# Feed-forward input stages with weights stationary and 256 tokens moving, for 18 of 22 weight groups

## The chip, the core and the metric

The kernel runs on one core of a Trainium2 chip. The metric is the device time of one execution in microseconds (us); three runs of the kernel before gave 941.71, 942.28 and 942.32 us, median 942.28.

## The reference

256 tokens of 1024 channels, all in float32, pass through a first block (feed-forward, token mixing by retention and neighbourhood attention, feed-forward) and a second block (a gated linear recurrence, a gated short convolution), with an RMS norm ahead of each part. The change touches the two feed-forward parts alone, which compute

```python
def _swiglu(x, w_in, w_out):
    g, u = jnp.split(x @ w_in, 2, axis=-1)
    return (jax.nn.silu(g) * u) @ w_out

for l in range(DEPTH):
    h = _swiglu(_rms_norm(x, ffn1_pre_norm[l]), ffn1_w_in[l], ffn1_w_out[l])
    x = x + 0.5 * _rms_norm(h, ffn1_post_norm[l])
    # token mixing
    h = _swiglu(_rms_norm(x, ffn2_pre_norm[l]), ffn2_w_in[l], ffn2_w_out[l])
    x = x + 0.5 * _rms_norm(h, ffn2_post_norm[l])
```

`w_in` is 1024 x 5632 (2816 gate columns and 2816 up columns) and `w_out` is 2816 x 1024.

## The kernel before

The program streams all weights once, in groups of 128 partitions x 2048 float32 (1 MB), through a ring of 4 slots. SyncE loads `raw`; ScalarE rounds it to `w_hi` (type fp32r); VectorE subtracts and gives `w_lo`. Every product of the large matrices is the sum of three matmuls in fp32r, hi times hi, hi times lo and lo times hi, so that the result keeps float32 precision. The normed tokens lie transposed in `xT_hi` and `xT_lo`, 8 blocks of 128 channels x 256 tokens.

In the feed-forward input stages (`f1_in`, `f2_in`, 22 groups each) two groups hold one column: 512 output columns (256 of the gate, 256 of the up part) over all 1024 channels. `column_tile` does one of the two halves of the tokens, t = 0 or 1, with 24 matmuls by `product`: a 128 x 128 piece of `xT` is the stationary operand and 512 columns of the weights move past it. So results stand in PSUM (`acc[:, t, par]`) with tokens on partitions. ScalarE takes silu of the gate half (`silu_g`), VectorE multiplies by the up half (`prod`), and because the next product needs the hidden channels on partitions, TensorE transposes `prod` with four 128 x 128 transposes per column (`hidden_transposes`, into the PSUM banks `aux`). ScalarE then rounds the transposed block to `hT_hi` and VectorE makes `hT_lo`. The output stages (`f1_out`, `f2_out`) use `hT` as stationary operand in the same way (`out_stage`).

All order is written by hand: each engine has its own program, and they meet at semaphores. A weight slot is given back to ScalarE when TensorE has used it (the table `RELEASE`), and the columns 2 to 9 of an input stage are a hardware loop of two columns per pass (`column`); column 10 follows outside it. TensorE starts a column tile once VectorE has emptied its PSUM bank two columns earlier, and does the transposes of the column before between the two tiles of a column. An input stage has 11 columns and 11 such bursts of four transposes; the last burst stands behind the first block of the output stage.

The weight load of a matmul is no instruction of the program here: the built rows show a matmul alone, the trace shows a LDWEIGHTS with each.

Of the kernel before, what the change touches and what calls it, by code (L numbers as in the profile page):

```python
# [53 lines left out]
ACC_READERS = {"f1_in": "V" * 11, "f1_out": "V", "mix_in": "AAAVVAAVVAAAA", "na_out": "V", "mix_out": "V",  # L54
               "f2_in": "V" * 11, "f2_out": "V", "a_in": "AAAVVV", "a_out": "V", "b_in": "V" * 12, "b_out": "V"}
ACC_ORDER = "".join(ACC_READERS.values())
FIRST_ACC = {}
for _name in ACC_READERS:
# [3 lines left out]
FILL_COUNTS = [("t0", 4), ("f1_in", 11), ("t1", 4), ("nq", 2), ("nk", 2), ("rq", 2), ("rk", 2), ("rs", 4), ("rp", 4),  # L62
               ("yna", 2), ("yret", 4), ("merged", 4), ("t2", 4), ("f2_in", 11), ("t3", 4),
# [3 lines left out]
SPLIT_COUNTS = [("t0", 4), ("f1_in", 11), ("t1", 4), ("yna", 2), ("yret", 4), ("merged", 4), ("t2", 4),  # L67
                ("f2_in", 11), ("t3", 4), ("gate", 6), ("t4", 4), ("b_in", 12)]
# [35 lines left out]
def build(nc, weights, x_in, gains, ident_in, rot_in, colmask_in, dist_in, decay_in, lam_in, bias_in, gate_w_in,  # L104
          gate_b_in, conv_a_in, conv_ab_in, conv_b_in, out):
    with ExitStack() as ctx:
# [60 lines left out]
        prod = at("prod", [P, 2, T, 256], F32, area + 47104)  # L167

# [53 lines left out]
        gate_ready = [sem(f"gate_ready{t}") for t in range(T)]  # L222
        bank_full = sem("bank_full")
# [59 lines left out]
        def act_frees(t, instruction):  # L283
            instruction.then_inc(acc_free_act[t], 1)

# [131 lines left out]
        def _(act):  # L417
# [4 lines left out]
            def round_group(g, slot=None, wait_used=True):  # L422
# [4 lines left out]
                if g >= RING:  # L427
                    kind, n = RELEASE[g - RING]
                    act.wait_ge({"used": group_used, "acc": acc_full[1], "ret": ret_acc_full}[kind], n)
# [7 lines left out]
            def round_in_loop(base_group, i, i0, b, per=4):  # L437
# [5 lines left out]
                act.wait_ge({"used": group_used, "acc": acc_full[1]}[kind], i * (per // 2) + (n - i0 * (per // 2)))  # L443
# [78 lines left out]
            def swiglu(which, normed):  # L522
# [16 lines left out]
                def column(j, par, rounds):  # L539
                    rounds()  # L540
                    silu(j, par, 0)
                    if not (isinstance(j, int) and j == 0):
                        hidden_hi(j - 1, 1 - par)
                    silu(j, par, 1)
# [17 lines left out]
                split[0] += 16  # L562
                column(10, 0, lambda: round_to(g0 + 24))
                round_to(g0 + 25)
                hidden_hi(10, 0)
# [9 lines left out]
            gates = [11, 11]  # L575
# [226 lines left out]
        def _(dve):  # L802
# [117 lines left out]
            def swiglu(which):  # L920
# [18 lines left out]
                def column(j, par, lows):  # L939
                    lows()  # L940
                    up(j, par, 0)
                    if not (isinstance(j, int) and j == 0):
                        hidden_lo(j - 1, 1 - par)
                    up(j, par, 1)
# [14 lines left out]
                with dve.Fori(1, 5) as i:  # L959
                    for b in range(2):  # L960
                        column(i * 2 + b, b, lambda: [low_in_loop(g0 + 6, i, 1, 2 * b + h) for h in range(2)])
                split[0] += 16
                column(10, 0, lambda: low_to(g0 + 24))
                low_to(g0 + 25)
                hidden_lo(10, 0)
                low_to(FIRST_GROUP[f"{which}_out"] + GROUPS[f"{which}_out"])

            GATES_F2 = 11 + 2
# [27 lines left out]
            for c in range(13):  # L996
                for t in range(T):
# [29 lines left out]
                    if c in (7, 8):  # L1027
                        dve.wait_ge(gate_ready[t], 11 + c - 6)
# [102 lines left out]
            gate0 = GATES_F2 + 11  # L1131
# [100 lines left out]
            gate0 = GATES_F2 + 11 + 3  # L1232
# [65 lines left out]
        def _(pe):  # L1298
# [64 lines left out]
            def out_stage(st, hi, lo, chunks, wait_chunk=lambda n: None, after_first=lambda: None, norm=None,  # L1363
                          last=3):
# [4 lines left out]
                for block in blocks:  # L1369
                    for t in range(T):  # L1370
                        if block[0] == 0:
                            wait_acc_free(pe, t, FIRST_ACC[st])
                        for n in block:
# [37 lines left out]
            def swiglu(which, n):  # L1411
# [26 lines left out]
                with pe.Fori(1, 5) as i:  # L1438
                    for b in range(2):
# [228 lines left out]
def _stream(inputs):  # L1668
# [6 lines left out]

    def rows(w):
        return w.reshape(-1, 2, P, DM).transpose(0, 2, 1, 3).reshape(-1, P, GROUP)

    def blocks(parts, width, at):
# [4 lines left out]
    ff = blocks((0, 1), 256, (0, FF))  # L1684
# [10 lines left out]
        columns(a["ffn1_w_in"][0], ff), rows(a["ffn1_w_out"][0]), columns(a["w_mix_in"][0], mix),  # L1695
        rows(a["w_na_out"][0]), rows(a["w_ret_out"][0]), rows(a["w_mix_out"][0]),
        columns(a["ffn2_w_in"][0], ff), rows(a["ffn2_w_out"][0]), columns(a["a_w_in_2"][0], a_cols),
# [62 lines left out]
```

## Time and profile before

| | |
|---|---|
| median of three runs | 942.28 us |
| profiled execution, first to last instruction | 940.6 us |
| TensorE matmul records, busy | 910.5 us, 97% |
| TensorE weight loads, busy (beside the matmuls) | 748.2 us, 80% |
| VectorE, ScalarE, GpSimd busy | 563.0, 451.7, 80.4 us |
| granted TensorE clock, mean over the span | 0.994 |
| HBM traffic | 167.61 MB read, 179 GB/s over the span |

The profile gives no time of the profiled execution other than its span; the runs' median lies 1.7 us above that span. In the timeline a row gives the start in us, the time to the end of the last instruction in it, the engine, the line, the operation with its tiles, and in brackets what it waited for. The end of a matmul is modelled and overlaps the next ones, so that the time of one matmul is read from the distance between two starts. PEld is the weight load; it has its own rows.

### The profile page before, as it was taken

The page shows a single profiled execution, that of the slowest core. Times are in us where ns is not written, and L with a number is a line of the kernel's source. Part 1 is how long each engine was busy: PE and PEld are TensorE (multiplying, and loading weights), DVE is VectorE, ACT ScalarE, POOL GpSimd, SP SyncE. Part 2 cuts the span into 40 slices and gives each one's busy share as a digit, 9 for nine tenths or more (in the row PEclk, how much of TensorE's full clock was granted, in tenths as well). Part 3 has the DMA queues.
Part 4 walks back from the last instruction along what each step waited for, and adds up shares of the span by engine and source line. Part 5 has one row for each costly group of instructions (what it writes and reads, how often), then busy time and mean ns, then how long its engine had stood idle before and what let it go on. Part 6 is the DMA issues. An engine that isn't in the chain of part 4 may idle for free.

```text
span 940.6 us, 11364 instructions
## 1 busy us (share of the span) xinstructions
PE 910.5 (97%) x4160; PEld 748.2 (80%) x4160; DVE 563.0 (60%) x625; ACT 451.7 (48%) x541; POOL 80.4 (9%) x107
## 2 busy tenths in 40 slices
PE   4999999999999999999999999999999799999997
PEld 3888888878888888888788888887887578888885
DVE  4755444466766556567655553555949866666653
ACT  5644444354533445436544443344877354444441
POOL 3000000003232200000000000000361200000000
PEclk9999999999999999999999999999999899999999
DMA  9744553637644443444544453755433454444421
GB/s 345 245 185 194 194 197 140 250 130 257 214 171 163 169 154 138 154 159 179 223 179 178 178 186 134 300 202 182 170 123 117 152 192 182 185 178 178 178 90 45
DMA packets 25684, 169.18 MB, mean 180 GB/s; under 512 B 3392, under 2 KB 3568, under 8 KB 6448
## 3 DMA queue, kind: packets, MB, share of 16 engines
q1 hardware_dynamic: 22752, 159.92, 45.7%
q0 software_dynamic: 2752, 8.69, 2.8%
q8 instruction: 25, 0.41, 0.2%
q14 instruction: 11, 0.09, 0.0%
q10 hardware_dynamic: 144, 0.07, 0.0%
HBM read 167.61 MB, written 1.05 MB: 179 GB/s over the span
## 4 chain that ended last, share of the span: by engine, by line
PE 89%; DVE 4%; ACT 3%; issue 2%; DMA 1%; SPq 0%; DVEq 0%; ACTq 0%
PE acc L1305 27%; PE acc L1307 26%; PE acc L1306 26%; DMA raw<-weights 1%; DVE w_lo L810 1%; PE aux L1425 1%; PE aux L1606 1%; PE aux L1358 1%; ACT w_hi L430 1%; PE aux L1306 1%; PE aux L1305 1%; PE aux L1307 1%; PE aux L1468 1%; PE aux L1518 1%; PE aux L1485 1%
## 5 line engine op out<-in xcount | busy, mean ns | idle before, releaser
L810 DVE TENSOR_TENSOR w_lo<-raw,w_hi 128x2048 fp32r<-128x2048 f32 x147 | 334.9, 2302 | 150.4 <-ACT w_hi L430 116.0
L1305 PE MATMUL acc<-w_hi,xT_hi 128*128 128x512 f32 x880 | 351.6, 400 | 6.0 <-DVE w_lo L810 3.0
L1307 PE MATMUL acc<-w_hi,xT_lo 128*128 128x512 f32 x880 | 344.7, 392 | 0.0
L1306 PE MATMUL acc<-w_lo,xT_hi 128*128 128x512 f32 x880 | 343.8, 391 | 0.0
L430 ACT ACTIVATE w_hi<-raw 128x2048 fp32r<-128x2048 f32 x97 | 184.0, 1912 | 91.1 <-PE acc L1307 75.9
L1305 PEld LDWEIGHTS acc<-w_hi,xT_hi 128*128 128x128 f32 x880 | 165.9, 188 | 41.3 <-DVE w_lo L810 4.7
L1307 PEld LDWEIGHTS acc<-w_hi,xT_lo 128*128 128x128 f32 x880 | 165.7, 188 | 35.8
L1306 PEld LDWEIGHTS acc<-w_lo,xT_hi 128*128 128x128 f32 x880 | 166.1, 189 | 32.8
L444 ACT ACTIVATE w_hi<-raw 128x2048 fp32r<-128x2048 f32 x52 | 96.6, 1910 | 0.9 <-issue 0.9
L532 ACT ACTIVATE silu_g<-acc 128x256 f32<-128x256 f32 x44 | 16.9, 383 | 121.5 <-PE acc L1307 121.5
L1305 PE MATMUL acc<-w_hi,hT_hi 128*128 128x512 f32 x176 | 69.8, 396 | 0.0
L1307 PE MATMUL acc<-w_hi,hT_lo 128*128 128x512 f32 x176 | 69.4, 395 | 0.0
L1306 PE MATMUL acc<-w_lo,hT_hi 128*128 128x512 f32 x176 | 69.4, 394 | 0.0
L930 DVE TENSOR_TENSOR prod<-acc,silu_g 128x256 f32<-128x256 f32 x44 | 18.5, 421 | 76.8 <-ACT silu_g L532 76.8
L1305 PE MATMUL acc<-w_hi,yT_hi 128*128 128x512 f32 x96 | 39.6, 413 | 5.8 <-DVE yT_lo L841 5.8
L1307 PEld LDWEIGHTS acc<-w_hi,hT_lo 128*128 128x128 f32 x176 | 33.2, 188 | 7.7
L1306 PEld LDWEIGHTS acc<-w_lo,hT_hi 128*128 128x128 f32 x176 | 33.2, 189 | 7.6
L1307 PE MATMUL acc<-w_hi,yT_lo 128*128 128x512 f32 x96 | 39.2, 408 | 0.0
L1305 PEld LDWEIGHTS acc<-w_hi,hT_hi 128*128 128x128 f32 x176 | 33.2, 188 | 7.5
L1306 PE MATMUL acc<-w_lo,yT_hi 128*128 128x512 f32 x96 | 39.1, 408 | 0.0
L581 ACT ACTIVATE prob<-neg_s,neg_max 128x256 f32<-128x256 f32 x16 | 8.2, 510 | 52.3 <-DVE neg_max L1067 41.6
L449 ACT ACTIVATE xT_hi<-aux 128x512 fp32r<-128x512 f32 x24 | 13.4, 596 | 33.9 <-PE aux L1358 28.6
(176 smaller groups left out, 774.2 us busy)
## 6 DMA issues: line engine op xcount, KB each, us to landing
raw<-weights SPq DMA_DIRECT2D x149, 1024.0 KB, 4.9
gain_pre<-gains POOLq DMA_DIRECT2D x5, 512.0 KB, 6.8
bias_raw<-bias_in POOLq DMA_DIRECT2D x32, 64.0 KB, 2.3
gain_post<-gains POOLq DMA_DIRECT2D x3, 512.0 KB, 6.1
gate_w<-gate_w_in POOLq DMA_DIRECT2D x1, 1536.0 KB, 7.0
x<-x_in SPq DMA_DIRECT2D x2, 512.0 KB, 8.0
raw<-weights SPq DMA_DIRECT2D x2, 512.0 KB, 7.8
out<-tmp SPq DMA_DIRECT2D x4, 256.0 KB, 2.1
```

The costliest lines, as they stand in the source:

```text
L430: a.activation(w_hi[:, slot], raw[:, slot], ACT.Copy).then_inc(hi_done, 1)
L444: a.activation(w_hi[:, slot], raw[:, slot], ACT.Copy).then_inc(hi_done, 1)
L449: a.activation(dst, source if source is not None else aux[:, bank], ACT.Copy, scale=scale)\
L532: a.activation(silu_g[:, t], acc[:, t, par, 0:256], ACT.Silu).then_inc(gate_ready[t], 1)
L810: v.tensor_tensor(w_lo[:, slot], raw[:, slot], w_hi[:, slot].bitcast(F32), ALU.subtract)\
L930: v.tensor_tensor(prod[:, par, t], acc[:, t, par, 256:512], silu_g[:, t], ALU.mult)\
L1305: m.matmul(dst, hi[:, k, cols], w_hi[:, slot, w], start=first, stop=False)
L1306: m.matmul(dst, hi[:, k, cols], w_lo[:, slot, w], start=False, stop=False)
L1307: return m.matmul(dst, lo[:, k, cols], w_hi[:, slot, w], start=False, stop=last)
L1358: i = m.transpose(aux[:, 2 * t + h, c * P:(c + 1) * P], tmp[:, t, (4 * h + c) * P:(4 * h + c + 1) * P], ident[:])
L1425: i = m.transpose(aux[:, par, c * S + t * P:c * S + (t + 1) * P], prod[:, par, t, c * P:(c + 1) * P], ident[:])
L1468: m.matmul(aux[:, 1, 0:S], nqT[h % 2][:, h // 2, t * P:(t + 1) * P], nkT[:, h // 2, :], start=True, stop=True).then_inc(s_full, 1)
```

## The change

The first 4 of the 22 groups (two columns) of each feed-forward input stage stay as they were (`STRAIGHT = 4`). The other 18 groups (`TURNED = 18`) are laid out anew in memory: a group now holds 128 gate columns and 128 up columns over all 1024 channels, a chunk. For a chunk TensorE takes a 128 x 128 piece of the weights as the stationary operand and lets the 256 tokens of `xT` move past it, 3 x 8 matmuls for the gate half and as many for the up half, both into one PSUM bank (`turned_bank`). The result has hidden channels on partitions. ScalarE takes silu (`silu_c`), VectorE multiplies (`prod_c`, in SBUF), ScalarE rounds `prod_c` to `hT_hi` and VectorE subtracts for `hT_lo`. No transposes are needed for these chunks. Four chunk banks take turns; a chunk waits for the product of the chunk four before it.

On TensorE, inside the loop of `f1_in`: before, the middle of one column (L1305 to L1307 are the three matmuls of `product`, L1425 the transposes)

```order
L1305 MATMUL acc<-w_hi,xT_hi 128x512
L1306 MATMUL acc<-w_lo,xT_hi 128x512
L1307 MATMUL acc<-w_hi,xT_lo 128x512
L1422 REGISTER_ALU
L1425 MATMUL aux<-ident,prod 128x128 x4
L1305 MATMUL acc<-w_hi,xT_hi 128x512
L1306 MATMUL acc<-w_lo,xT_hi 128x512
L1307 MATMUL acc<-w_hi,xT_lo 128x512
```

and now, the end of one chunk and the start of the next (L1507 to L1509 are the three matmuls of `turned_chunk`)

```order
L1507 MATMUL acc<-xT_hi,w_hi 128x256
L1508 MATMUL acc<-xT_lo,w_hi 128x256
L1509 MATMUL acc<-xT_hi,w_lo 128x256
L1497 REGISTER_ALU
L1501 REGISTER_ALU
L1507 MATMUL acc<-xT_hi,w_hi 128x256
L1508 MATMUL acc<-xT_lo,w_hi 128x256
L1509 MATMUL acc<-xT_hi,w_lo 128x256
```

The transposes are gone from the loop, and a group has 48 matmuls of 256 columns where it had 24 of 512. On ScalarE the loop of `f1_in` holds, before, for one column (two groups)

```order
L444 ACTIVATE w_hi<-raw 128x2048 x2
L529 REGISTER_ALU
L532 ACTIVATE silu_g<-acc 128x256
L535 REGISTER_ALU
L537 ISA
L537 ACTIVATE hT_hi<-aux 128x512
L532 ACTIVATE silu_g<-acc 128x256
```

and now, for two chunks (two groups)

```order
L465 ACTIVATE w_hi<-raw 128x2048
L567 ACTIVATE silu_c<-acc 128x256
L574 ISA
L574 ACTIVATE hT_hi<-prod_c 128x256
L465 ACTIVATE w_hi<-raw 128x2048
L567 ACTIVATE silu_c<-acc 128x256
L574 ISA
L574 ACTIVATE hT_hi<-prod_c 128x256
```

One rounding of 512 columns out of PSUM has become two of 256 out of SBUF; VectorE's loop changes in the same way. The diff, without the counts of semaphores that follow from it:

```diff
+STRAIGHT = 4
+TURNED = 18
+TURNED_BEFORE = {"f1_in": 0, "f2_in": TURNED}
 ...
-        if _name.endswith("_in") and _g % 2 or _name.endswith("_out") and _g == _n - 1:
+        if _name in TURNED_BEFORE and _g >= STRAIGHT:
+            RELEASE.append(("turned", TURNED_BEFORE[_name] + _g - STRAIGHT + 1))
+        elif _name.endswith("_in") and _g % 2 or _name.endswith("_out") and _g == _n - 1:
 ...
+        def turned_bank(b):
+            return acc[:, 1 - b % 4 // 2, b % 2]
 ...
+                def chunk_silu(n, b):
+                    act.wait_ge(turned_full, n + (c_before + 1))
+                    if not (isinstance(n, int) and n < 2):
+                        act.wait_ge(prod_ready, n + (c_before - 1))
+                    a.activation(silu_c[:, b % 2], turned_bank(b)[:, 0:S], ACT.Silu).then_inc(silu_ready, 1)
+
+                def chunk_round(n, b):
+                    act.wait_ge(prod_ready, n + (c_before + 1))
+                    ...
+                    a.activation(dst, prod_c[:, b % 2], ACT.Copy).then_inc(chunk_hi, 1)
 ...
-                with act.Fori(1, 5) as i:
-                    for b in range(2):
-                        column(i * 2 + b, b, lambda: [round_in_loop(g0 + 6, i, 1, 2 * b + h) for h in range(2)])
+                with act.Fori(1, 4) as i:
+                    for b in range(4):
+                        round_in_loop(g0 + 10, i, 1, b)
+                        chunk_silu(i * 4 + b, b)
+                        chunk_round(i * 4 + (b - 1), b + 3)
 ...
+                def chunk_up(n, b):
+                    dve.wait_ge(silu_ready, n + (c_before + 1))
+                    ...
+                    v.tensor_tensor(prod_c[:, b % 2], turned_bank(b)[:, S:2 * S], silu_c[:, b % 2], ALU.mult)\
+                        .then_inc(prod_ready, 1)
+
+                def chunk_low(n, b):
+                    dve.wait_ge(chunk_hi, n + (c_before + 1))
+                    ...
+                    v.tensor_tensor(dst, prod_c[:, b % 2], hi.bitcast(F32), ALU.subtract).then_inc(chunk_lo, 1)
 ...
-                def column(j, par):
-                    for t in range(T):
-                        pe.wait_ge(acc_free_dve[t], n_dve - 1 + j)
-                        column_tile(g0 + 2 * j, (g0 + 2 * par) % RING, par, t)
-                        if t == 0:
-                            hidden_transposes(j - 1, 1 - par)
+                def turned_chunk(c, b):
+                    pe.wait_ge(lo_done, c + (g0 + STRAIGHT + 1))
+                    if isinstance(c, int) and c < 4:
+                        pe.wait_ge(acc_free_dve[1 - c // 2], n_dve + 1 + c % 2)
+                    else:
+                        pe.wait_ge(prod_ready, c + (c_before - 3))
+                    slot = (g0 + STRAIGHT + b) % RING
+                    for half in range(2):
+                        dst = turned_bank(b)[:, half * S:(half + 1) * S]
+                        for k in range(KD):
+                            w = slice(2 * P * k + P * half, 2 * P * k + P * (half + 1))
+                            m.matmul(dst, w_hi[:, slot, w], xT_hi[:, k, :], start=k == 0, stop=False)
+                            m.matmul(dst, w_hi[:, slot, w], xT_lo[:, k, :], start=False, stop=False)
+                            i = m.matmul(dst, w_lo[:, slot, w], xT_hi[:, k, :], start=False, stop=k == KD - 1)
+                    i.then_inc(turned_full, 1)
 ...
-                with pe.Fori(1, 5) as i:
-                    for b in range(2):
-                        column(i * 2 + b, b)
-                column(10, 0)
+                for c in range(4):
+                    turned_chunk(c, c)
+                    if c == 0:
+                        hidden_transposes(1, 1)
+                with pe.Fori(1, 4) as i:
+                    for b in range(4):
+                        turned_chunk(i * 4 + b, b)
+                for c in range(16, TURNED):
+                    turned_chunk(c, c)
 ...
-                    pe.wait_ge(bank_free, f0 + g + 1)
-
-                out_stage(f"{which}_out", hT_hi, hT_lo, FF // P, wait_chunk, lambda: hidden_transposes(10, 0),
-                          n + 1, 4)
+                    if g < STRAIGHT // 2:
+                        pe.wait_ge(bank_free, f0 + g + 1)
+                    else:
+                        pe.wait_ge(chunk_lo, c_before + 2 * g - STRAIGHT + 2)
+
+                def free_banks(t):
+                    pe.wait_ge(prod_ready, c_before + (TURNED if t else TURNED - 2))
+
+                out_stage(f"{which}_out", hT_hi, hT_lo, FF // P, wait_chunk, lambda: None, n + 1, 4, free_banks)
```

## Rows read from the trace of the kernel before

**Rows 1.** The page: busy time by engine, granted TensorE clock, last chain by engine.

```profile
PE 910.5 (97%) x4160; PEld 748.2 (80%) x4160; DVE 563.0 (60%) x625; ACT 451.7 (48%) x541; POOL 80.4 (9%) x107
PEclk9999999999999999999999999999999899999999
PE 89%; DVE 4%; ACT 3%; issue 2%; DMA 1%; SPq 0%; DVEq 0%; ACTq 0%
```

**Rows 2.** All that TensorE waited for: us in total, times, longest us.

```profile
PE aux L1358 <- DVE tmp L878: 9.3, 3, 8.0
PE acc L1305 <- DVE yT_lo L841: 5.8, 2, 3.8
PE acc L1305 <- DVE w_lo L810: 3.0, 3, 1.0
PE acc L1305 <- DVE w_lo L826: 3.0, 1, 3.0
PE aux L1595 <- DVE a_stage L1183: 2.1, 1, 2.1
```

**Rows 3.** Timeline of TensorE, transposes of successive columns: f1_in, then f2_in (columns as above).

```profile
56.96 0.60 PE L1425 MATMUL aux<-ident,prod 128*128 128x128 f32 x4
68.33 0.60 PE L1425 MATMUL aux<-ident,prod 128*128 128x128 f32 x4
...
136.57 0.60 PE L1425 MATMUL aux<-ident,prod 128*128 128x128 f32 x4
...
472.18 0.60 PE L1425 MATMUL aux<-ident,prod 128*128 128x128 f32 x4
...
563.16 0.60 PE L1425 MATMUL aux<-ident,prod 128*128 128x128 f32 x4
```

**Rows 4.** Timeline of TensorE, matmuls of 512 columns ahead of and behind a burst.

```profile
99.73 0.39 PE L1305 MATMUL acc<-w_hi,xT_hi 128*128 128x512 f32 x1
...
102.45 0.60 PE L1425 MATMUL aux<-ident,prod 128*128 128x128 f32 x4
102.81 0.48 PE L1305 MATMUL acc<-w_hi,xT_hi 128*128 128x512 f32 x1
103.12 0.40 PE L1306 MATMUL acc<-w_lo,xT_hi 128*128 128x512 f32 x1
```

**Rows 5.** Timeline of the weight loads (PEld) around the same burst.

```profile
102.22 0.58 PEld L1425 LDWEIGHTS aux<-ident,prod 128*128 128x128 f32 x4
102.78 0.19 PEld L1305 LDWEIGHTS acc<-w_hi,xT_hi 128*128 128x128 f32 x1
102.89 0.19 PEld L1306 LDWEIGHTS acc<-w_lo,xT_hi 128*128 128x128 f32 x1
103.12 0.19 PEld L1307 LDWEIGHTS acc<-w_hi,xT_lo 128*128 128x128 f32 x1
```

**Rows 6.** Timeline of TensorE, 16 transposes in a row, in mix_in.

```profile
375.95 1.04 PE L1459 MATMUL aux<-ident,y_na 128*128 128x128 f32 x8
376.83 1.04 PE L1459 MATMUL aux<-ident,y_ret 128*128 128x128 f32 x8
```

**Rows 7.** Timeline of TensorE, 8 passes of a plain float32 matmul of 256 columns.

```profile
330.71 1.89 PE L1518 MATMUL aux<-rv,decay 128*128 128x256 f32 x8
332.44 0.59 PE L1468 MATMUL aux<-nkT,nqT 128*128 128x256 f32 x2
```

**Rows 8.** Timeline of the weight loads, matmuls of 64 columns, then the first of 512.

```profile
260.58 0.53 PEld L1485 LDWEIGHTS aux<-nv,probT 128*128 128x128 f32 x4
261.03 0.19 PEld L1305 LDWEIGHTS acc<-w_hi,xT_hi 128*128 128x128 f32 x1
```

**Rows 9.** Timeline of TensorE in f1_out, at 512 columns: the first and twelfth of twelve.

```profile
157.58 0.39 PE L1305 MATMUL acc<-w_hi,hT_hi 128*128 128x512 f32 x1
...
160.13 0.40 PE L1307 MATMUL acc<-w_hi,hT_lo 128*128 128x512 f32 x1
```

**Rows 10.** Groups by line, 45.6 to 136.5 us: busy, mean ns | idle before.

```profile
L810 DVE TENSOR_TENSOR w_lo<-raw,w_hi 128x2048 fp32r<-128x2048 f32 x17 | 38.2, 2288 | 12.3 <-ACT w_hi L444 10.9 <-ACT w_hi L430 1.4
L444 ACT ACTIVATE w_hi<-raw 128x2048 fp32r<-128x2048 f32 x14 | 26.0, 1908 | 0.9 <-issue 0.9
L1306 PEld LDWEIGHTS acc<-w_lo,xT_hi 128*128 128x128 f32 x128 | 24.1, 188 | 4.8
L930 DVE TENSOR_TENSOR prod<-acc,silu_g 128x256 f32<-128x256 f32 x16 | 6.7, 421 | 31.8 <-ACT silu_g L532 31.8
L532 ACT ACTIVATE silu_g<-acc 128x256 f32<-128x256 f32 x16 | 6.1, 383 | 48.6 <-PE acc L1307 48.6
L936 DVE TENSOR_TENSOR hT_lo<-aux,hT_hi 128x512 f32 x8 | 5.4, 680 | 0.0
L537 ACT ACTIVATE hT_hi<-aux 128x512 f32 x8 | 4.8, 598 | 1.3 <-PE aux L1425 1.3
```

More of the change, by code:

```diff
@@ L167, in build @@
         prod = at("prod", [P, 2, T, 256], F32, area + 47104)
+        silu_c = at("silu_c", [P, 2, S], F32, area + 51200)
+        prod_c = at("prod_c", [P, 2, S], F32, area + 53248)
         nqT = [at(f"nqT{i}", [P, NH // 2, S], F32, area + 4096 * i) for i in range(2)]
@@ L428, in round_group @@
                     kind, n = RELEASE[g - RING]
[L429 removed]
+                    act.wait_ge({"used": group_used, "acc": acc_full[1], "ret": ret_acc_full,
+                                 "turned": turned_full}[kind], n)
                 a.activation(w_hi[:, slot], raw[:, slot], ACT.Copy).then_inc(hi_done, 1)
@@ L442, in round_in_loop @@
                 kind, n = RELEASE[base_group + b - RING]
-                act.wait_ge({"used": group_used, "acc": acc_full[1]}[kind], i * (per // 2) + (n - i0 * (per // 2)))
+                each = per if kind == "turned" else per // 2
+                act.wait_ge({"used": group_used, "acc": acc_full[1], "turned": turned_full}[kind],
+                            i * each + (n - i0 * each))
                 a.activation(w_hi[:, slot], raw[:, slot], ACT.Copy).then_inc(hi_done, 1)
@@ L537, in hidden_hi @@
                     a.activation(dst, aux[:, par].rearrange("p (c q) -> p c q", c=2), ACT.Copy).then_inc(bank_hi, 1)
[L539 to L544, printed above, removed]
+                c_before = TURNED_BEFORE[st]
+                def chunk_silu(n, b):
[5 more added lines that the diff above has]
+                    act.wait_ge(prod_ready, n + (c_before + 1))
+                    dst = hT_hi[:, STRAIGHT + n, :] if isinstance(n, int) else \
+                        hT_hi[:, bass.ds(n + STRAIGHT, 1), :].rearrange("p a q -> p (a q)")
+                    a.activation(dst, prod_c[:, b % 2], ACT.Copy).then_inc(chunk_hi, 1)
                 if g0 == 0:
@@ L937, in hidden_lo @@
                                     hT_hi[:, chunks, :].bitcast(F32), ALU.subtract).then_inc(bank_free, 1)
[L939 to L944, printed above, removed]
+                c_before = TURNED_BEFORE[st]
+                def chunk_up(n, b):
+                    dve.wait_ge(silu_ready, n + (c_before + 1))
+                    if not (isinstance(n, int) and n < 2):
+                        dve.wait_ge(chunk_lo, n + (c_before - 1))
+                    v.tensor_tensor(prod_c[:, b % 2], turned_bank(b)[:, S:2 * S], silu_c[:, b % 2], ALU.mult)\
+                        .then_inc(prod_ready, 1)
+                def chunk_low(n, b):
+                    dve.wait_ge(chunk_hi, n + (c_before + 1))
+                    dst, hi = (hT_lo[:, STRAIGHT + n, :], hT_hi[:, STRAIGHT + n, :]) if isinstance(n, int) else \
+                        [x[:, bass.ds(n + STRAIGHT, 1), :].rearrange("p a q -> p (a q)") for x in (hT_lo, hT_hi)]
+                    v.tensor_tensor(dst, prod_c[:, b % 2], hi.bitcast(F32), ALU.subtract).then_inc(chunk_lo, 1)
                 if g0 == 0:
@@ L958, in swiglu @@
                 hidden_lo(0, 0)
-                with dve.Fori(1, 5) as i:
-                    for b in range(2):
-                        column(i * 2 + b, b, lambda: [low_in_loop(g0 + 6, i, 1, 2 * b + h) for h in range(2)])
-                split[0] += 16
-                column(10, 0, lambda: low_to(g0 + 24))
+                for n in range(4):
+                    low_to(g0 + 7 + n)
+                    chunk_up(n, n)
+                    if n == 0:
+                        hidden_lo(1, 1)
+                    else:
+                        chunk_low(n - 1, n - 1)
+                with dve.Fori(1, 4) as i:
+                    for b in range(4):
+                        low_in_loop(g0 + 10, i, 1, b)
+                        chunk_up(i * 4 + b, b)
+                        chunk_low(i * 4 + (b - 1), b + 3)
+                split[0] += 12
+                for n in range(16, TURNED):
+                    low_to(g0 + 7 + n)
+                    chunk_up(n, n)
+                    chunk_low(n - 1, n - 1)
+                chunk_low(TURNED - 1, TURNED - 1)
                 low_to(g0 + 25)
-                hidden_lo(10, 0)
                 low_to(FIRST_GROUP[f"{which}_out"] + GROUPS[f"{which}_out"])
-            GATES_F2 = 11 + 2
+            GATES_F2 = 2 + 2
             swiglu("f1")
@@ L1674, in columns, with chunks @@
         return w.reshape(-1, P, GROUP)
+    def chunks(w, order):
+        w = w.reshape(KD, P, -1)[:, :, order]
+        return w.transpose(2, 1, 0, 3).reshape(-1, P, GROUP)
     def rows(w):
```

54 lines of the change are left out of this document (36 added, 18 removed).

## The prediction, made before the result was known

> **What bounds the kernel now.** I read the page first. TensorE's matmul records cover 97% of the span and make up 89% of the chain that ended last [rows 1]. The list of its waits comes to 23 us in the whole kernel, and none of it is in the part of the feed-forward input stages that changes: its largest entries belong to the norms (L1358), to the recurrence (L841) and to the start (L826) [rows 2]. The groups by line for the loop of `f1_in` say the same from the other side: VectorE and ScalarE sit idle there for silu and for matmul results, 48.6 us before silu alone in 91 us, and no TensorE group idles [rows 10]. So inside these stages the time is a count of TensorE instructions times their pitch, the distance between two starts. Everything else only has to keep up.
>
> The pitch is what one must read with care. A matmul record of 512 columns is 390 ns long, but twelve of them start in 2.72 us (99.73 to 102.45), so the pitch is 227 ns [rows 4]. The granted clock is at its upper level, 2.4 GHz, in the feed-forward stages [rows 1], where 512 columns are 213 ns; 13 ns per matmul are something else. The same holds for the weight load: its record is 188 ns long [rows 10], yet loads follow each other faster than that (below).
>
> **What is removed and added on TensorE.** A column (two groups) takes 11.37 us: the bursts at 56.96 and 68.33 are that far apart, those from 56.96 to 136.57 are 7 x 11.37, and in the second stage 472.18 to 563.16 is 8 x 11.37 [rows 3]. 48 matmuls at 227 ns are 10.88 us of it; the other 0.49 us is the burst of four transposes with what it upsets: 0.36 us from its start to the next matmul's record, and 0.31 instead of 0.23 us from there to the one after [rows 4]. Nine columns of each stage are turned, and nine bursts of each go (the burst of column 1 stays, that of column 10 behind the first output block goes). Old time of what is replaced: 9 x 11.37 = 102.35 us per stage, 4.4 of it bursts.
>
> New time: 18 chunks x 48 = 864 matmuls of 256 columns per stage, each with a weight load of its own (the three rows of a chunk show the same slice of `w_hi` used twice in a row; the trace of before has a load record for every matmul, 4160 and 4160 [rows 1], although `xT_hi` is used twice in a row there too, so none will be saved). With a pitch p a stage takes 864 p. The change breaks even at p = 102.35 / 864 = 118.5 ns. This is the whole question: the same number of columns moves as before, but the fixed part of a matmul and the weight load are paid twice as often, against 4.4 us of bursts.
>
> **Bounds of p.** No fp32r matmul of 256 columns is in the trace. From below: weight loads limit it. Behind matmuls of 64 columns loads start every 112 ns (four from 260.58 to 261.03) [rows 8]; an fp32r load behind a short matmul is followed by the next after 0.11 us (102.78, 102.89) [rows 5]; 16 transposes keep 0.11 us each (8 from 375.95 to 376.83) [rows 6]. So p is at least 110 to 112 ns: now 0.23 us of matmul hides a load of 0.11, then they are about equal. That the load runs beside the matmul before it is seen in rows 5: the load at 102.89 starts as the matmul whose own load began at 102.78 begins, and the next matmul starts only at 103.12. From the matmul's side: 256 columns are 107 ns at 2.4 GHz. If the 13 ns grow with the columns (17/16 of 512), p is 113 ns; if they are paid per matmul, 120 ns. In the output stage the same shape has a pitch of 232 ns (eleven starts in 2.55 us), 19 ns extra [rows 9], which speaks for a cost per matmul that depends on what surrounds it, and would give 126 ns. From above: eight passes of plain float32 with 256 columns take 1.73 us, 216 ns each [rows 7], and the load's record is 188 ns [rows 10]; both would be reached only if a load could no more run beside the short matmul ahead of it, which rows 6 and 8 speak against.
>
> I take 120 ns: the extra varies between 13 and 19 ns at one and the same column count, so it is not a share of the columns, and plain float32, where the array needs two steps per column (216 for 213 ns), hardly shows it, so it is something of the full-rate stream at each start. Sum: 864 x 0.120 = 103.7 us against 102.35, +1.35 per stage, +2.7 us for both.
>
> A page of the Trainium skill, "TensorE: Matmul & The Clock Gate" (Back-to-back issue gap), gives the gap as columns / 2.4 plus 2.5 ns. The plain float32 rows agree (216); the fp32r rows do not (227 where it says 216), and the measurement decides. Its section LDWEIGHTS gives columns / 1.2, 107 ns for 128, and the rows above show 108 to 112.
>
> **The rest of the change.** VectorE per group: 2.29 + 0.42 for the product, and for `hT_lo` at most 0.68, its price for twice the elements: 3.4 us of a chunk of 5.4 to 5.8. ScalarE: 1.91 + 0.38 + at most 0.60 = 2.9 us [rows 10]. Both have cover, so I cost them at nothing; if the cover were gone, the excess over 5.7 us would be paid 36 times. The waits added: TensorE waits for the product of the chunk four before, whose silu and product (0.8 us plus what is queued ahead, one rounding or subtraction of 1.9 to 2.3) had three chunks, 17 us. The slot of a group is released when its chunk ends, and rounding 1.91 and subtracting 2.29 have three chunks too; queued behind it on ScalarE is the silu of a chunk that TensorE is still in. At the end of the stage the last chunk's bank is needed by t = 1 of the output stage, after 24 matmuls, 5.4 us, against about 1 us of silu and product, or 3.5 us if a subtraction stands ahead. SyncE's loads wait for `lo_done` as before, and the bytes are the same. Bound on all this: 0 to +2 us for a wait at the four seams, and to -1.3 us per output stage if its 232 ns fell to 227 for want of transposes (264 x 5 ns) [rows 9]; I take 0.
>
> 940.6 + 2.7 = 943.3 us of span, and with the 1.7 us between span and median of the runs, 945.0 us. I call changes within 0.2% (1.9 us) no difference, about what a measurement can tell.
>
> **Rivals.**
> First, the extra is not paid per matmul: a load and a matmul of about equal length run side by side and p is 110 to 116 ns. For it: loads and transposes do reach 110 to 112 [rows 5, 6, 8], and the 13 ns are exactly 1/16 of 213. Against it: rows 9. At 113.3 ns a stage takes 97.9 us, -4.4 each, 933.5 us; at 110, 95.0, -7.3 each, 927.7 us.
> The skill's gap rule (same page and section as above) says 109 ns for 256 columns; this rival is that rule with the load's limit from the rows.
>
> Second, p is larger, 123 to 135 ns: the load starts when the matmul ahead starts and needs 112 ns, and the extra of 13 to 19 ns comes behind whichever is later. For it: with both lengths near 110 there is no slack left between them, and [rows 9] show the larger extra for a whole stage of 512-column matmuls. It decides from p = 123 on. At 126 ns: 108.9 us, +6.5 each, 955.3 us; at 135 ns (112 and the larger extra, and a little): 116.6, +14.3 each, 970.9 us.
>
> Third, the short matmul hides no load, or TensorE's instruction supply falls behind over 864 in a row (the longest run of short ones in the trace is 16 [rows 6]): 188 ns gives 162.4, +60 each, 1062 us; 216 ns gives 186.6, 1111 us. The same page (Wait — 56ns, not 53.3ns?) has about 62 ns of sequencer time per MATMUL with hardware decode off; two instructions would be 124 ns, an estimate that falls in the second rival. No run here shows it.
>
> **How the numbers follow.** Forecast, 117.3 to 123 ns: 0.40, of which 0.10 falls within 0.2% (117.3 to 119.6 ns) and 0.30 above. First rival: 0.36, all faster. Second: 0.20. Third: 0.04. So faster 0.36, same 0.10, slower 0.54. The range leaves out the third rival, the far end of the second beyond 131 ns and the end of the first below 113: 932 to 964 us. The likeliest case alone is 940 to 950.
>
> **What would show it.** In the profile after, the pitch of `turned_chunk`'s matmuls: 24 of one half in 2.88 us, a chunk every 5.76 us. 5.4 us or less is the first rival, over 5.9 the second. The load records of these matmuls should start when the matmul ahead starts. Bursts of `prod` should be 16 instructions in all for the two stages, where there were 88. A wait of TensorE on `silu_c`, `prod_c` or `w_lo` of over 2 us in all in these stages would prove the costing of the rest wrong. I am wrong in sign if p is under 117.3 ns, and wrong in mechanism if TensorE idles between chunks.

## The result: 2.6 us slower, at the forecast pitch of 120 ns

The changed kernel takes 945.13 us (median of 19 runs, 944.28 to 947.64), the kernel before in the same comparison 942.55 us. The ratio is 1.0028, 95% interval 1.0021 to 1.0034. The forecast was 945.0 us. The profiled execution has a span of 942.9 us against 940.6.

The page of the changed kernel, busy time by engine, where [rows 1] stand for before:

```profile
PE 912.7 (97%) x4952; PEld 786.5 (83%) x4952; DVE 569.9 (60%) x643; ACT 452.4 (48%) x559; POOL 80.5 (9%) x107
```

There are 792 more matmuls and 792 more loads: 864 added (24 more for each of 36 groups), 72 transposes gone. TensorE has as few gaps as before. All its waits in the changed kernel (us in total, times, longest):

```profile
PE aux L1421 <- DVE tmp L919: 9.3, 3, 8.1
PE acc L1368 <- DVE yT_lo L882: 5.8, 2, 3.8
PE acc L1368 <- DVE w_lo L851: 3.1, 3, 1.1
PE acc L1368 <- DVE w_lo L867: 3.0, 1, 3.0
PE aux L1681 <- DVE a_stage L1246: 2.1, 1, 2.1
```

These are [rows 2] under new line numbers. No wait on a chunk's product or silu has come. So the whole difference must lie in TensorE's own work, the pitch of the new matmuls against that of the old ones and the bursts. The timeline of TensorE inside a chunk of `f1_in`, its first and ninth row of nine:

```profile
79.96 0.28 PE L1507 MATMUL acc<-xT_hi,w_hi 128*128 128x256 f32 x1
...
80.92 0.28 PE L1509 MATMUL acc<-xT_hi,w_lo 128*128 128x256 f32 x1
```

Eight distances in 0.96 us are 120.0 ns each. The weight loads keep the same beat and start with the matmul ahead of them, back to back (timeline of the loads, changed kernel):

```profile
79.96 0.19 PEld L1508 LDWEIGHTS acc<-xT_lo,w_hi 128*128 128x128 f32 x1
80.08 0.19 PEld L1509 LDWEIGHTS acc<-xT_hi,w_lo 128*128 128x128 f32 x1
```

Stage by stage, from the first burst to the first matmul of the output stage. Before, in `f1` and then in `f2`:

```profile
39.65 0.60 PE L1425 MATMUL aux<-ident,prod 128*128 128x128 f32 x4
...
142.51 0.40 PE L1305 MATMUL acc<-w_hi,hT_hi 128*128 128x512 f32 x1
...
466.24 0.60 PE L1425 MATMUL aux<-ident,prod 128*128 128x128 f32 x4
...
569.10 0.40 PE L1305 MATMUL acc<-w_hi,hT_hi 128*128 128x512 f32 x1
```

and in the changed kernel:

```profile
39.50 0.60 PE L1489 MATMUL aux<-ident,prod 128*128 128x128 f32 x4
...
144.04 0.39 PE L1368 MATMUL acc<-w_hi,hT_hi 128*128 128x512 f32 x1
...
467.37 0.60 PE L1489 MATMUL aux<-ident,prod 128*128 128x128 f32 x4
...
571.90 0.39 PE L1368 MATMUL acc<-w_hi,hT_hi 128*128 128x512 f32 x1
```

Second stage: 102.86 us before, 104.53 us after, +1.67. The first stage is the same (39.65 to 142.51, 39.50 to 144.04: +1.68). The last burst stood behind this point and is gone too, 0.49 us per stage. 2 x (1.67 - 0.49) = 2.4 us, against the span's 2.3.

### The profile page after: what moved, and what is told of

Read it like the earlier page. It is cut to its first block, busy times and chain, and to the rows that moved or that the text cites. A ratio compares the mean times of both kernels' runs of the same rounds, so it can differ in the third digit from the quotient of the medians.

```text
span 942.9 us, 12924 instructions
## 1 busy us (share of the span) xinstructions
PE 912.7 (97%) x4952; PEld 786.5 (83%) x4952; DVE 569.9 (60%) x643; ACT 452.4 (48%) x559; POOL 80.5 (9%) x107
## 4 chain that ended last, share of the span: by engine, by line
PE 89%; DVE 4%; ACT 3%; issue 2%; DMA 1%; SPq 0%; DVEq 0%; ACTq 0%
PE acc L1368 20%; PE acc L1370 19%; PE acc L1369 19%; PE acc L1508 7%; PE acc L1507 7%; PE acc L1509 7%; DMA raw<-weights 1%; DVE w_lo L851 1%; PE aux L1692 1%; PE aux L1421 1%; ACT w_hi L449 1%; PE aux L1368 1%; PE aux L1370 1%; PE aux L1369 1%; PE aux L1554 1%
## 5 line engine op out<-in xcount | busy, mean ns | idle before, releaser
L1368 PE MATMUL acc<-w_hi,xT_hi 128*128 128x512 f32 x592 | 237.4, 401 | 6.1 <-DVE w_lo L851 3.1
L1370 PE MATMUL acc<-w_hi,xT_lo 128*128 128x512 f32 x592 | 232.0, 392 | 0.0
L1369 PE MATMUL acc<-w_lo,xT_hi 128*128 128x512 f32 x592 | 231.6, 391 | 0.0
L1507 PE MATMUL acc<-xT_hi,w_hi 128*128 128x256 f32 x576 | 163.3, 284 | 0.0
L1509 PE MATMUL acc<-xT_hi,w_lo 128*128 128x256 f32 x576 | 163.0, 283 | 0.0
L1508 PE MATMUL acc<-xT_lo,w_hi 128*128 128x256 f32 x576 | 163.0, 283 | 0.0
L1368 PEld LDWEIGHTS acc<-w_hi,xT_hi 128*128 128x128 f32 x592 | 111.8, 189 | 30.8 <-DVE w_lo L851 4.9
L1369 PEld LDWEIGHTS acc<-w_lo,xT_hi 128*128 128x128 f32 x592 | 111.9, 189 | 22.0
L1508 PEld LDWEIGHTS acc<-xT_lo,w_hi 128*128 128x128 f32 x576 | 110.6, 192 | 0.0
L1507 PEld LDWEIGHTS acc<-xT_hi,w_hi 128*128 128x128 f32 x576 | 110.6, 192 | 0.0
L1509 PEld LDWEIGHTS acc<-xT_hi,w_lo 128*128 128x128 f32 x576 | 110.6, 192 | 0.0
```

The lines of the kernel that those rows point to most:

```text
L1368: m.matmul(dst, hi[:, k, cols], w_hi[:, slot, w], start=first, stop=False)
L1369: m.matmul(dst, hi[:, k, cols], w_lo[:, slot, w], start=False, stop=False)
L1370: return m.matmul(dst, lo[:, k, cols], w_hi[:, slot, w], start=False, stop=last)
L1507: m.matmul(dst, w_hi[:, slot, w], xT_hi[:, k, :], start=k == 0, stop=False)
L1508: m.matmul(dst, w_hi[:, slot, w], xT_lo[:, k, :], start=False, stop=False)
L1509: i = m.matmul(dst, w_lo[:, slot, w], xT_hi[:, k, :], start=False, stop=k == KD - 1)
```

## The experiments

Twelve kernels ran. They ask three things: whether each half of the sum has its size; what the 13 ns per matmul are; and why the same shape runs at 227 ns in one stage and 232 in another, on which the choice of 120 ns rested.

**The gain half alone.** The kernel before without nine bursts per stage; their waits and their signal stay:

```diff
-                        column_tile(g0 + 2 * j, (g0 + 2 * par) % RING, par, t)
-                        if t == 0:
-                            hidden_transposes(j - 1, 1 - par)
+                        column_tile(g0 + 2 * j, (g0 + 2 * par) % RING, par, t,
+                                    in_last=(lambda: hidden_waits(j - 1)) if t == 0 else None)
 ...
```

> The kernel before, in which the nine bursts of four transposes of the loop and column 10 of each feed-forward input stage are left out and only their waits and their signal remain (so the hidden layer of these columns is not right). This is the gain half of the change alone. My sum: 9 x 0.49 us per stage, 8.8 us in all, a ratio of 0.9906. Rival: the transposes fill time that TensorE would otherwise spend waiting for silu and product, so that less than half of it comes back: 0.995 or above. Second rival: only the array time of the transposes goes (36 x 0.107 per stage, 7.7 us) and the longer pitch behind them stays: 0.992.

933.83 us, ratio 0.9907 (0.9891 to 0.9924): 8.8 us, the size of my sum. 0.995 lies outside the interval, so the transposes did not fill idle time. The second rival's 0.992 lies inside it, but the trace tells the two apart. ScalarE's `silu_g` comes twice per column; its first and seventeenth row in the loop of `f1_in`, in this run:

```profile
45.70 0.38 ACT L532 ACTIVATE silu_g<-acc 128x256 f32<-128x256 f32 x1 [1.29 <-PE acc L1307]
...
132.74 0.38 ACT L532 ACTIVATE silu_g<-acc 128x256 f32<-128x256 f32 x1 [1.43 <-PE acc L1307]
```

Eight columns take 87.04 us, 10.88 each, where it was 11.37 [rows 3]. A burst was thus worth 0.49 us, as in my sum, and not only the 0.43 us of its four transposes (4 x 0.107).

The cost half follows: 1.0028 / 0.9907 = 1.0122, 11.4 us, where my sum has 2 x (103.68 - 97.9) = 11.5 us. The change is thus a trade of 11.4 against 8.8 us.

**Width of the moving operand, below 256.** In `turned_chunk`, `n` is 240 in the gate half and 192 in the up half:

```diff
+                        n = (240, 192)[half]
 ...
-                            m.matmul(dst, w_hi[:, slot, w], xT_hi[:, k, :], start=k == 0, stop=False)
+                            m.matmul(dst, w_hi[:, slot, w], xT_hi[:, k, 0:n], start=k == 0, stop=False)
 ...
```

> The changed kernel, with the moving operand of a chunk's matmuls cut to 240 of the 256 tokens in the gate half and to 192 in the up half (the last tokens of the hidden layer are left out, so the output is not the reference's). Theory A, a fixed 13.3 ns per fp32r matmul on top of columns / 2.4: 100.0 + 13.3 = 113.3 ns pitch at 240 columns; at 192 it would be 93.3, under the 110 to 112 ns that loads take, so 112 ns. Theory B, the 120 ns is the weight load (112 ns) plus a hand-over of 8 ns and has nothing to do with the columns: 120 ns at both. Theory C, the extra is a share of the columns plus the same load floor: 112 at both.

Timeline of TensorE in this run, the first and last row of 16 at 192 columns, then of 12 at 240:

```profile
60.17 0.27 PE L1510 MATMUL acc<-xT_hi,w_lo 128*128 128x192 f32 x1
...
61.85 0.28 PE L1510 MATMUL acc<-xT_hi,w_lo 128*128 128x192 f32 x1
...
62.20 0.27 PE L1510 MATMUL acc<-xT_hi,w_lo 128*128 128x240 f32 x1
...
63.43 0.28 PE L1509 MATMUL acc<-xT_lo,w_hi 128*128 128x240 f32 x1
```

112.0 ns at 192 columns and 111.8 at 240. Both lie at the distance of loads, 112 ns, and below 120, so the load is not what makes 120 (theory B falls). At 240 columns C said 112 and A 113.3. A is missed by 1.5 ns, more than the rounding of the two starts can make (0.9 ns): the 13.3 ns do not hold so close to the distance of loads.

**Width above 256.** The same with 320 and 384 columns.

> The changed kernel, with the moving operand of a chunk's matmuls made 320 columns wide in the gate half and 384 in the up half (they run into the next block of channels, and overlap in the PSUM bank, so the output is not the reference's). Theory A, 13.3 ns per matmul: 133.3 + 13.3 = 146.7 ns at 320 and 160 + 13.3 = 173.3 ns at 384. Theory C, 1/16 of the columns: 141.7 and 170.0 ns. Theory B (at 256 the load limits, and from some width on the columns): 142 to 147 and 170 to 173, it does not differ here. The span grows by 1728 matmuls x 40 ns = 69 us under A (mean pitch 160 against 120).

Timeline of this run, 18 rows at 384 columns and 20 at 320, first and last:

```profile
60.30 0.33 PE L1511 MATMUL acc<-xT_hi,w_hi 128*128 128x384 f32 x1
...
63.25 0.33 PE L1513 MATMUL acc<-xT_hi,w_lo 128*128 128x384 f32 x1
...
64.00 0.31 PE L1512 MATMUL acc<-xT_lo,w_hi 128*128 128x320 f32 x1
...
66.79 0.31 PE L1513 MATMUL acc<-xT_hi,w_lo 128*128 128x320 f32 x1
```

173.5 and 146.8 ns, where A had 173.3 and 146.7, and C 170.0 and 141.7. C falls here. Its 113 ns at 256 columns, one form of the prediction's first rival, had fallen with the measured 120.0. With a full load and the operands where they are, an fp32r matmul of 256, 320, 384 or 512 columns costs its columns at 2.4 GHz and 13.3 ns.

**Length of the load.** 64 of 128 weight columns as stationary operand, 256 and 192 columns moving:

```diff
-                        dst = turned_bank(b)[:, half * S:(half + 1) * S]
+                        n = (S, 192)[half]
+                        dst = turned_bank(b)[0:64, half * S:half * S + n]
 ...
-                            w = slice(2 * P * k + P * half, 2 * P * k + P * (half + 1))
+                            w = slice(2 * P * k + P * half, 2 * P * k + P * half + 64)
 ...
```

> The changed kernel, with 64 instead of 128 weight columns as stationary operand (64 of the 128 channels of each chunk are left out), 256 tokens moving in the gate half and 192 in the up half. The load is half as long. Theory A, the extra belongs to the start of the moving stream: 120.0 ns at 256 columns as before, and 80 + 13.3 = 93.3 ns at 192, since the load's floor falls from 112 to about 56 ns. Theory B, the pitch of 120 is load plus hand-over: both fall well under 120, to 107 to 110 at 256 columns and 80 to 83 at 192. Theory D, the extra is the load disturbing the stream beside it: it halves, 113.3 and 86.7 ns.

Timeline of this run, 21 rows at 192 columns, then 17 at 256, first and last:

```profile
60.24 0.25 PE L1508 MATMUL acc<-xT_hi,w_hi 128*64 128x192 f32 x1
...
62.01 0.25 PE L1510 MATMUL acc<-xT_hi,w_lo 128*64 128x192 f32 x1
...
62.92 0.28 PE L1509 MATMUL acc<-xT_lo,w_hi 128*64 128x256 f32 x1
...
64.73 0.28 PE L1510 MATMUL acc<-xT_hi,w_lo 128*64 128x256 f32 x1
```

88.5 and 113.1 ns. This is not A (93.3 and 120.0): of the 13.3 ns, 8.5 are left at 192 columns and 6.4 at 256, near theory D's 86.7 and 113.3. Two more runs tried D. The first takes 32 and 96 stationary columns at 256 moving; the second is the kernel before, with 64 token columns stationary in the groups that its hardware loop issues:

```diff
+                        rows = (32, 96)[half]
 ...
+                            w = slice(2 * P * k + P * half, 2 * P * k + P * half + rows)
```

```diff
+                        n = P if isinstance(g, int) else 64
 ...
+                        slot, cols, dst = (slot0 + half) % RING, slice(t * P, t * P + n), acc[0:n, t, par]
 ...
```

> The changed kernel, 256 tokens moving, with 32 stationary weight columns in the gate half and 96 in the up half (the other channels are left out). In the run with 64 stationary columns the pitch at 256 columns was 113.3 ns, at 128 it is 120.0. Theory D, the extra grows with the load's columns, 32 clock steps for 128: 32 columns 110.0 ns, 96 columns 116.7 ns. Rival, the extra comes in two steps (a short load gives 113.3, a long one 120.0): 113.3 and 120.0.

> The kernel before, in which the matmuls of the looped columns (columns 2 to 9 of the two feed-forward input stages, 2 to 11 of b_in; 1248 matmuls of 512 columns) have 64 instead of 128 stationary columns, so that half of the tokens' results in them are left out. It carries the finding of the run with half loads to the unturned form. Theory D, a load takes 32 clock steps from the stream it runs beside, a half load 16: the pitch falls from 226.7 to 220.0 ns, the span by 1248 x 6.7 = 8.3 us. Theory A, the extra is a start cost that only looked smaller in the short matmuls: 226.7 stays, and so does the span.

Timeline of the first of these runs, 21 rows with 96 stationary columns, then 21 with 32, first and last:

```profile
60.76 0.28 PE L1508 MATMUL acc<-xT_hi,w_hi 128*96 128x256 f32 x1
...
63.08 0.27 PE L1510 MATMUL acc<-xT_hi,w_lo 128*96 128x256 f32 x1
...
63.55 0.28 PE L1508 MATMUL acc<-xT_hi,w_hi 128*32 128x256 f32 x1
...
65.90 0.28 PE L1510 MATMUL acc<-xT_hi,w_lo 128*32 128x256 f32 x1
```

With 32 stationary columns the pitch was 117.5 ns, with 96 it was 116.0. D said 110.0 and 116.7, its rival 113.3 and 120.0; neither has both. In the unturned form with half loads the pitch rose, and the span with it, to 943.4 us (one run; the kernel before had 940.0 to 941.9 in the same comparison):

```profile
61.31 0.39 PE L1327 MATMUL acc<-w_hi,xT_lo 128*64 128x512 f32 x1
...
64.08 0.39 PE L1327 MATMUL acc<-w_hi,xT_lo 128*64 128x512 f32 x1
```

12 distances in 2.77 us are 231 ns, where D wanted 220 and A 227. Over the whole run the mean distance is 230.1 ns with half loads and 227.8 with full ones. D falls as a rule, and A with it as an explanation: the extra depends on the stationary operand in a way that neither describes.

**Order and banks in the output stages.** `out_tile` with `half` as the outer loop (six matmuls in a row to one PSUM bank), and then 12 to 24 in a row by taking groups in pairs:

```diff
-                for kk in range(2):
-                    ...
-                    for half in range(2):
+                for half in range(2):
+                    ...
+                    for kk in range(2):
```

> The kernel before, with the output tiles' matmuls ordered so that six in a row go to one PSUM bank where it was three. The question is why the output stages run at 232 ns where the input stages run at 227 with the same shapes. Theory bank: each change of the PSUM bank costs about 17 ns spread over what follows, so half the changes give 2.8 ns per matmul over 1056 matmuls, -3.0 us, ratio 0.997. Rival, the upset lasts for about ten matmuls behind a change (as it does behind a burst of transposes) and six in a row are still all upset: 0 to -0.5 us, ratio 1.000.

> The kernel before, with output groups taken in pairs and the PSUM bank changed once per pair of groups (12 in a row, 24 in the last block of four groups; 6 in na_out, ret_out and mix_out). Theory bank with a fixed cost per change: -4.5 us, ratio 0.995. Theory bank with an upset of some ten matmuls (about 50 ns in all): 12 in a row 231 ns, 24 in a row 229 ns, -1.5 us, ratio 0.998. Rival, the pitch has nothing to do with the banks: the pitch stays at 232. Taking groups in pairs releases slots later and could add a wait for w_lo: +1 us at most.

Six in a row: ratio 1.0003 (0.9994 to 1.0012), where the theory of banks had 0.997. Pairs of groups: 1.0245 (1.0231 to 1.0259), and the pitch has not moved, 13 rows in the last block of `f1_out`:

```profile
185.73 0.39 PE L1307 MATMUL acc<-w_hi,hT_lo 128*128 128x512 f32 x1
...
188.52 0.39 PE L1307 MATMUL acc<-w_hi,hT_lo 128*128 128x512 f32 x1
```

2.79 us / 12 = 232.5 ns. The banks are out. My estimate of +1 us for the later release of slots was far off. TensorE's waits in this run add up to 39.6 us instead of 23.2 [rows 2], the largest of them

```profile
PE aux L1360 <- DVE tmp L878: 15.1, 5, 8.1
PE acc L1305 <- DVE w_lo L810: 7.9, 5, 3.5
```

and the mean granted clock is 0.986 instead of 0.994. Both together are of the size of the 22.8 us; I have not separated them.

**Where the stationary operand lies.** `mix_out` is ordered as the output stages are but has `xT` as stationary operand, and runs at 227. One number changed in the kernel before:

```diff
-        area = cursor[0]
+        area = cursor[0] + (base - cursor[0]) % 2048
```

> The kernel before with one number changed: the area in which hT, yT, yretT and ynaT lie starts 128 bytes later, on a multiple of 2048 bytes from the first tensor, as xT does. The order of matmuls and the PSUM banks have been ruled out as the reason why the output stages run at 232 ns and the input stages at 227; mix_out, which is ordered as they are but has xT as stationary operand, runs at 227. Theory address: where the stationary operand lies decides; the 960 matmuls with hT, yT, yretT and ynaT fall to 227 ns, 960 x 5.6 = -5.4 us, ratio 0.9943. Rival: something else about these stages (waits, the two other engines) sets the pitch: 1.000.

937.15 us, ratio 0.9936 (0.9922 to 0.9949). Timeline of TensorE in `f1_out` of this run, first and last of 16, to be held against [rows 9]:

```profile
157.06 0.39 PE L1305 MATMUL acc<-w_hi,hT_hi 128*128 128x512 f32 x1
...
160.46 0.39 PE L1305 MATMUL acc<-w_hi,hT_hi 128*128 128x512 f32 x1
```

226.7 ns. Over the whole run the matmuls with `hT` have a mean distance of 226.9 ns, where it was 232.4. The cross-check moves `xT` off its place and, with it, the area onto one:

```diff
+        cursor[0] += 128
         xT_hi = sb("xT_hi", [P, KD, S], F32R)
```

> The kernel before with 128 bytes left free ahead of xT_hi. xT (and x, the gains, the constants) now begin 128 bytes off a multiple of 2048 bytes from the first tensor, and the area of hT, yT, yretT and ynaT comes to lie on such a multiple. The weights, the moving operand, stay where they are. Theory address, of the stationary operand: the two kinds of stages change places. Input stages and mix_out go from 226.7 to about 232 ns (2640 + 96 matmuls, +15.3 us), the other output stages from 232 to 226.7 (960, -5.4 us): +10 us, ratio 1.0105. Rival, only the area's own place mattered (for instance by what VectorE and ScalarE read and write there): input stages stay at 227 and the ratio is 0.994 as in the aligned run.

950.27 us, ratio 1.0080 (1.0063 to 1.0097). The 1.0105 expected lies outside: over the whole run the matmuls with `xT` went from a mean distance of 227.8 ns to 232.9, 5.1 ns more and not 5.6, which is part of the shortfall. The stages have changed places. Timeline of this run, ten rows in `f1_in`, then 13 in `f1_out`:

```profile
23.75 0.39 PE L1308 MATMUL acc<-w_hi,xT_lo 128*128 128x512 f32 x1
...
25.84 0.40 PE L1308 MATMUL acc<-w_hi,xT_lo 128*128 128x512 f32 x1
...
165.07 0.39 PE L1307 MATMUL acc<-w_lo,hT_hi 128*128 128x512 f32 x1
...
167.79 0.39 PE L1307 MATMUL acc<-w_lo,hT_hi 128*128 128x512 f32 x1
```

232 ns in the input stage, 226.7 in the output stage. A stationary operand 128 bytes off its multiple costs 5 to 6 ns per matmul, in both directions and with the moving operand untouched. No other offset was tried. The pieces themselves start every 512 bytes from the start of their tensor, so the multiple that counts need not be 2048.

**A version that beats both.** The turned form pays 13.3 ns for each matmul, so it should issue fewer. `w_hi` is stationary for both the hi and the lo tokens: one matmul of 512 columns does the work of two of 256. The lo results land beside the hi results, ScalarE copies them out and VectorE adds them.

```diff
-                            m.matmul(dst, w_hi[:, slot, w], xT_hi[:, k, :], start=k == 0, stop=False)
-                            m.matmul(dst, w_hi[:, slot, w], xT_lo[:, k, :], start=False, stop=False)
-                            i = m.matmul(dst, w_lo[:, slot, w], xT_hi[:, k, :], start=False, stop=k == KD - 1)
 ...
+                            i = m.matmul(dst, w_hi[:, slot, w], xT_both[:, :, k, :], start=k == 0, stop=k == KD - 1)
+                            if k < KD - 1:
+                                m.matmul(dst[:, 0:S], w_lo[:, slot, w], xT_hi[:, k, :], start=False, stop=False)
```

> A version meant to beat both kernels. The turned chunks take w_hi as stationary operand against the tokens' hi and lo parts in one matmul of 512 columns (hi results in columns 0 to 255 of a PSUM bank, lo results in 256 to 511), and w_lo against the hi part in one of 256; 32 matmuls and 32 loads per chunk where there were 48. ScalarE copies the lo results out, VectorE adds them (four more short operations per chunk), and a chunk holds two banks, so that two chunks take turns where it was four. Theory, 13.3 ns on each matmul: a chunk takes 16 x (226.7 + 120.0) = 5.55 us against 5.76 in the changed kernel and 5.69 per group with bursts in the kernel before; 18 x 5.55 = 99.8 us per stage against 102.35, -5.0 us, 937.5 us, ratio 0.9947. Rival, the wide matmuls fall into the longer pitch of 232 ns: 100.7 per stage, -3.3 us, 0.9965. Second rival, with two chunks instead of four TensorE waits for the products: VectorE needs 3.9 us of a chunk and the way from a full chunk to its product has five steps, some 2.5 us, of 5.5 there are; a wait of 0.5 us per chunk would cost 18 us, ratio 1.013.

941.36 us, ratio 0.9987 (0.9978 to 0.9996): faster than before, by a quarter of what was expected. No wait on a chunk appeared, so the second rival is out. The pitch of a pair was 350 to 353 ns instead of 346.7, as in the first rival. Its sum was wrong, though: 288 pairs of 352 ns are 101.4 us per stage, not 100.7, and that gives a ratio of 0.998, which the interval holds. Timeline, four pairs in 1.40 us:

```profile
62.51 0.28 PE L1524 MATMUL acc<-xT_both,w_lo 128*128 128x256 f32 x1
...
63.91 0.28 PE L1524 MATMUL acc<-xT_both,w_lo 128*128 128x256 f32 x1
```

The last version adds the shift of the area to this and sorts a chunk's matmuls, the wide ones first:

```diff
+        area = cursor[0] + (base - cursor[0]) % 2048
 ...
+                    for wide in (True, False):
```

> The version with hi and lo tokens in one matmul of 512 columns, with the same shift of the area, and with the matmuls of a chunk sorted: first its 16 wide ones, then its 16 short ones. In the run with wide and short taking turns a pair took about 353 ns instead of 346.7, and ratios came to 0.9987. Theory: alternating widths keep the stream in its longer pitch, equal widths in a row settle at 226.7 and 120.0; a chunk takes 5.55 to 5.60 us, -4 to -5 us against before without the shift, and with the shift -5 more if the address matters: 932 to 934 us, ratio 0.990. If only one of the two holds 0.995. Rival, neither: 0.999.

932.82 us, ratio 0.9896 (0.9880 to 0.9912), the best version of this study, 1.3% under the changed kernel. Timeline of TensorE, one chunk from its wide matmuls to the next chunk's:

```profile
62.74 3.82 PE L1522 MATMUL acc<-xT_both,w_hi 128*128 128x512 f32 x16
66.40 2.08 PE L1524 MATMUL acc<-xT_both,w_lo 128*128 128x256 f32 x16
68.31 3.82 PE L1522 MATMUL acc<-xT_both,w_hi 128*128 128x512 f32 x16
```

5.57 us per chunk: 16 wide ones in 3.66 us (229 ns), 16 short ones in 1.91 (119). Both parts of the theory held, the wide ones at 229 ns where it had 226.7. The shift alone had 0.9936, so the fused and sorted chunk is worth about 0.9896 / 0.9936 = 0.996, which no run measured by itself.

## Why the prediction was right

**Bound.** TensorE's count times its pitch bound these stages and still does. Waits before and after are the same list.

**Gain half.** 0.49 us per burst, 8.8 us in all. The run without bursts measured both.

**Cost half.** 120 ns was the forecast and 120.0 the measurement. The sum had +1.33 us per stage; the stages show 1.67 to the end of the input stage and 1.18 with the last burst taken off, 0.15 us less than the sum. Twice that is most of the distance between the span's +2.3 us and the +2.7 forecast. Where it comes from no run tells.

**The rest at nothing.** Held: no new wait. VectorE's total rose by 6.9 us to 569.9, and no wait of TensorE came of it. The allowance of -1.3 us per output stage, for want of transposes, was wrong in its reason: the output stages' 232 ns do not come from bursts but from where `hT` lies, and they stayed.

**The choice between 113 and 120 ns.** Its conclusion was right, and neither of its two reasons was what I took it for. I argued that the extra cannot be a share of the columns because it is 13 ns in one stage and 19 in another. The runs at 320 and 384 columns show that it is no share. But the step from 13 to 19 ns comes from the address of the stationary operand, which says nothing on that question. So the argument did not exclude 113 ns, and that 120 came out was in this part luck. The second reason, a cost of the full-rate stream at each start, is not shown either: the extra changes with the number of stationary columns. The turned form had 13.3 ns and not 19. Its stationary operand, the weights, lies at offsets that are multiples of 512 bytes, which would account for it. Had it lain as `hT` does, the second rival's 126 ns would have been near. Both are inferences: no run moved the weights.

**The rivals.** The first was given 0.36 and is refuted by the 120.0 ns of the changed kernel; the two runs with wider operands refute its share of the columns. The distance of loads that it leaned on is real (112 ns at 192 and 240 columns) and lies 8 ns below. The second and third did not happen: behind the last burst of a stage 816 short matmuls ran in a row without a gap.

**Still open.** What the 13.3 ns are. They are the same at four widths under a full load (256, 320, 384 and 512 columns). At 256 columns moving they are 6.4 ns under a load of 64 columns, 10.8 under 32 and 9.3 under 96, and at 512 columns moving 17 to 18 ns under a load of 64. Why alternating widths cost 3 to 6 ns per pair, and equal ones behind a change settle only after some matmuls, is open too.

## What to carry to other kernels

Where TensorE is the bound, count matmuls and not only columns: in fp32r each one here cost 13.3 ns beyond its columns at 256 columns and more, under a full weight load, and none had a pitch below the 112 ns from one such load to the next. 256-column matmuls give up 6% against 512-column ones before anything is gained. Read the pitch from starts, stage by stage; if the same shape has two pitches in one kernel, look at the addresses of the operands before the order of the work. An elimination that trades long matmuls for short ones has to be priced as the difference of two large numbers (here 11.4 against 8.8 us), and fusing two products that share a stationary operand gets part of the price back.

## What the runs showed of the hardware

- The start address of the stationary operand changes the pitch of 512-column fp32r matmuls: 226.7 ns where its tensor starts on a multiple of 2048 bytes from the first tensor, 232 to 233 ns where it starts 128 bytes beside such a place. 128 bytes of padding were worth 0.64% of this kernel, more than the change under study.
- Loads of 128 float32 columns beside short fp32r matmuls started 112 ns apart, though the record of one is 188 to 192 ns long; a matmul of 192 columns gained nothing in pitch over one of 240 (112.0 and 111.8 ns). With loads of 64 columns the pitch at 192 was 88.5 ns.
- Half a weight load (64 columns) lowers the pitch of short matmuls (113.1 instead of 120.0 ns at 256 columns), and raises that of long ones (231 instead of 227 ns at 512 in a settled stretch, 230.1 instead of 227.8 over a whole run).
- Matmuls of 512 and 256 columns taking turns took 350 to 353 ns per pair; sorted by width, 16 of each in a row, they took 229 + 119 = 348 ns.
